# Seven block products in place of eight in the second feed-forward layer of a decoder block

## What is computed

```python
h2 = rms_norm(x, norm2_g[l])
x = x + jnp.square(jax.nn.relu(h2 @ w_ff1[l])) @ w_ff2[l]    # w_ff1 1024 x 4096, w_ff2 4096 x 1024
```

## Time and profile before

| | |
|---|---|
| median of 3 runs | 461.83 us (461.47 to 462.28) |
| the profiled execution itself | 461.82 us, span 459.7 us |
| PE busy | 452.8 us, 99% |
| DVE busy | 314.0 us, 68% |
| ACT busy | 239.2 us, 52% |
| POOL busy | 35.0 us, 8% |
| granted TensorE clock | 1.0 of full speed throughout |

### The profile page before, as it was taken

The page is one execution under the profiler, slowest core; times in us unless marked ns, Lnnn a source line. Parts: engine busy times, 40 slices in busy tenths (PEclk is TensorE's granted clock), DMA queues, the critical chain, the costliest instruction groups (busy, mean ns, idle before and its releaser), DMA issues.

```text
span 459.7 us, 8210 instructions
## 1 busy us (share of the span) xinstructions
PE 452.8 (99%) x3392; PEld 380.5 (83%) x3392; DVE 314.0 (68%) x438; ACT 239.2 (52%) x355; POOL 35.0 (8%) x44
## 2 busy tenths in 40 slices
PE   7999999999999999999999999999999999999997
PEld 4999988789977777878888888888888888888885
DVE  3868799675374867676688858766666666666662
ACT  5868584655565556666533547444444444444430
POOL 3003000023580001002000000000000000000000
PEclk9999999999999999999999999999999999999999
DMA  8973645433524434446656564656566555566402
GB/s 273 320 243 105 228 138 180 143 97 96 177 66 131 135 112 152 129 131 184 195 175 198 169 201 151 194 185 186 188 194 199 191 185 186 194 193 197 145 1 91
DMA packets 49076, 76.55 MB, mean 167 GB/s; under 512 B 3088, under 2 KB 29456, under 8 KB 49040
## 3 DMA queue, kind: packets, MB, share of 16 engines
q1 hardware_dynamic: 49040, 76.03, 53.1%
HBM read 74.97 MB, written 1.05 MB: 165 GB/s over the span
## 4 chain that ended last, share of the span: by engine, by line
PE 92%; DVE 4%; DMA 1%; ACT 1%; issue 1%; SPq 0%
PE bank L504 21%; PE bank L506 20%; PE bank L505 20%; PE bank L555 13%; PE bank L557 6%; DMA stage<-in_w_in 1%; PE bank L752 1%; PE bank L771 1%; PE bank L656 1%; DVE w_lo L1168 1%; DVE mat L1273 1%; DVE mat L1288 1%; DVE xs L1499 1%; PE bank L847 1%; PE bank L811 1%
## 5 line engine op out<-in xcount | busy, mean ns | idle before, releaser
L1168 DVE TENSOR_TENSOR w_lo<-stage,w_hi 128x1024 fp32r<-128x1024 f32 x138 | 167.6, 1223 | 82.7 <-ACT w_hi L918 82.5
L918 ACT CAST w_hi<-stage 128x1024 fp32r<-128x1024 f32 x138 | 144.1, 1052 | 126.3 <-PE bank L506 74.1
L555 PE MATMUL bank<-h_two,w_hi 128*128 128x512 f32 x256 | 91.2, 399 | 0.3 <-DVE h_two L1419 0.3
L557 PE MATMUL bank<-h_two,w_lo 128*128 128x256 f32 x256 | 71.8, 281 | 0.0
L504 PE MATMUL bank<-w_hi,h_two 128*128 128x512 f32 x144 | 59.8, 415 | 0.0
L555 PEld LDWEIGHTS bank<-h_two,w_hi 128*128 128x128 f32 x256 | 48.1, 188 | 12.3 <-issue 0.6
L504 PE MATMUL bank<-w_hi,r_hi 128*128 128x512 f32 x144 | 56.4, 392 | 0.0
L505 PE MATMUL bank<-w_lo,h_two 128*128 128x512 f32 x144 | 56.4, 391 | 0.0
L506 PE MATMUL bank<-w_hi,h_two 128*128 128x512 f32 x144 | 56.4, 391 | 0.0
L505 PE MATMUL bank<-w_lo,r_hi 128*128 128x512 f32 x144 | 56.2, 390 | 0.0
L506 PE MATMUL bank<-w_hi,r_lo 128*128 128x512 f32 x144 | 56.0, 389 | 0.0
(11 more groups left out here) (245 smaller groups left out, 630.5 us busy)
## 6 DMA issues: line engine op xcount, KB each, us to landing
stage<-in_w_ff SPq DMA_DIRECT2D x64, 512.0 KB, 3.7
stage<-in_w_in SPq DMA_DIRECT2D x54, 512.0 KB, 4.4
stage<-in_w_branch SPq DMA_DIRECT2D x12, 512.0 KB, 4.3
stage<-in_w_out SPq DMA_DIRECT2D x8, 512.0 KB, 4.4
xs<-in_x SPq DMA_DIRECT2D x2, 512.0 KB, 4.0
out<-xs SPq DMA_DIRECT2D x4, 256.0 KB, 2.1
cst<-in_consts SPq DMA_DIRECT2D x1, 608.0 KB, 6.0
lora<-in_g_up SPq DMA_DIRECT2D x1, 256.0 KB, 6.0
```

What stands on the lines that cost most here:

```text
L555: pe.matmul(o[:].rearrange("p (s t) -> p s t", s=2), wh[:, kk, cols], h_two[:, :, k], start=k == 0, stop=False)
L557: ins = pe.matmul(o[:, T:2 * T], wl[:, kk, cols], h_hi[:, k], start=False, stop=k == KD - 1)
L918: nc.scalar.copy(w_hi[:, v % RING], stage[:, v % STAGES]).then_inc(hi_done, 1)
L1168: dve.tensor_tensor(w_lo[:, v % RING], stage[:, v % STAGES], w_hi[:, v % RING].bitcast(F32), ALU.subtract)\
```

## The change

All 16 ff1 units now come first; their squared results all stay in SBUF (`fsq` has 16 buffers). Then come the 16 steps of the second layer. In seven of them (i = 0, 2, ... 12) the 2 x 2 by 2 x 2 block product is made by Winograd's form of Strassen's method, with seven block products and sums of blocks of both factors; such a step is two units, `("seven", i, 0)` and `("seven", i, 1)`, with four pieces. The first two are the loaded rows of `w_ff2` (of the first only half the columns is split), the other two (`SUMS`) are sums of weight blocks in the buffer `w_sum`, which isn't loaded but made by GpSimd. The other nine steps are as before. Products add up in eight PSUM banks, and DVE combines those after step 12.

The core of the diff:

```diff
-UNITS += [("ff1", 0)]
-for i in range(1, D_FF // 256):
-    UNITS += [("ff1", i), ("ff2", i - 1)]
-UNITS += [("ff2", D_FF // 256 - 1)]
+FF = D_FF // 256
+SEVEN = list(range(0, FF - 2, 2))
+UNITS += [("ff1", i) for i in range(FF)]
+for i in range(FF):
+    UNITS += [("seven", i, 0), ("seven", i, 1)] if i in SEVEN else [("ff2", i)]
...
+                if s >= STAGES:
+                    freed = LOADS[s - STAGES]
+                    sp.wait_ge(lo_done, freed + 1)
+                    if UNITS[freed // 2][0] == "seven":
+                        sp.wait_ge(wsum_ready, 4 * SEVEN.index(UNITS[freed // 2][1]) + 4)
...
+                elif u[0] == "seven":
+                    buf = 4 * (u[1] % 2)
+                    if u[2] == 0 and p == 0:
+                        pe.wait_ge(f_ready, SPLITS[u[1]])
+                    work = {(0, 1): ("M1", 0, 0, 0), (0, 2): ("M2", 1, 0, 0), (0, 3): ("M3", 3, 1, 1),
+                            (1, 0): ("M5", 2, 0, 0), (1, 1): ("M6", 2, 1, 1), (1, 2): ("M7", 3, 0, 0),
+                            (1, 3): ("M4", 1, 1, 1)}.get((u[2], p))
...
+            def gain(tt, c, ap):
+                xc = xs[:, tt, 512 * c:512 * c + 512]
+                return dve.scalar_tensor_tensor(out=xc, in0=ap, scalar=r2[:, tt:tt + 1], in1=xc, op0=ALU.mult, op1=ALU.add)\
+                          .then_inc(x_part, 1)
...
+                if (t, p) == (FF2_AT[SEVEN[-1] + 1], 2):
+                    dve.wait_ge(used, 2 * t)
+                    link(dve.tensor_copy(msum[0], ps(("mlp", "M1"))[:]))
+                    link(dve.tensor_tensor(msum[1], msum[0], ps(("mlp", "M6"))[:], ALU.add))
+                    link(dve.tensor_tensor(msum[2], msum[1], ps(("mlp", "M7"))[:], ALU.add))
+                    gain(0, 0, msum[0])
+                if (t, p) == (FF2_AT[SEVEN[-1] + 2], 2):
+                    dve.tensor_tensor(msum[3], msum[1], ps(("mlp", "M5"))[:], ALU.add).then_inc(tail_sum, 1)
+                    dve.tensor_tensor(msum[4], msum[2], ps(("mlp", "M5"))[:], ALU.add).then_inc(tail_sum, 1)
+                    gain(1, 0, msum[2])
+                    dve.wait_ge(tail_sum, 2)
+                    gain(0, 1, msum[3])
+                    gain(1, 1, msum[4])
...
+            for n, i in enumerate(SEVEN):
+                pool.wait_ge(sq_ready, i + 1)
+                if n >= 2:
+                    pool.wait_ge(f_ready, SPLITS[SEVEN[n - 2]])
+                a11, a21, a12, a22 = (fsq[i][:, P * b:P * b + P] for b in range(4))
+                s1, s2, s3, s4 = (a_sum[n % 2][:, P * b:P * b + P] for b in range(4))
+                pool.tensor_tensor(s1, a21, a22, ALU.add).then_inc(asum_ready, 1)
+                pool.tensor_tensor(s3, a11, a21, ALU.subtract).then_inc(asum_ready, 1)
+                pool.wait_ge(asum_ready, 4 * n + 2)
+                pool.tensor_tensor(s2, s1, a11, ALU.subtract).then_inc(asum_ready, 1)
+                pool.wait_ge(asum_ready, 4 * n + 3)
+                pool.tensor_tensor(s4, a12, s2, ALU.subtract).then_inc(asum_ready, 1)
+                v = 2 * FF2_AT[i]
+                if n >= 2:
+                    pool.wait_ge(lo_done, 2 * FF2_AT[SEVEN[n - 2]] + 4)
+                landed(pool, v)
+                landed(pool, v + 1)
+                b11, b12, b21, b22 = (source(v + r)[:, 512 * c:512 * c + 512] for r in range(2) for c in range(2))
+                t1, t2, t3, t4 = (w_sum[:, n % 2, r, 512 * c:512 * c + 512] for r in range(2) for c in range(2))
+                pool.tensor_tensor(t1, b12, b11, ALU.subtract).then_inc(wsum_ready, 1)
+                pool.wait_ge(wsum_ready, 4 * n + 1)
+                pool.tensor_tensor(t2, b22, t1, ALU.subtract).then_inc(wsum_ready, 1)
+                pool.tensor_tensor(t3, b22, b12, ALU.subtract).then_inc(wsum_ready, 1)
+                pool.wait_ge(wsum_ready, 4 * n + 2)
+                pool.tensor_tensor(t4, b21, t2, ALU.subtract).then_inc(wsum_ready, 1)
```

More of the change, by code:

```diff
@@ L65 @@
 UNITS += [("out", kh, ch) for kh in range(2) for ch in range(2)]
-UNITS += [("ff1", 0)]
-for i in range(1, D_FF // 256):
-    UNITS += [("ff1", i), ("ff2", i - 1)]
-UNITS += [("ff2", D_FF // 256 - 1)]
+FF = D_FF // 256
[3 more added lines that the diff above has]
+    UNITS += [("seven", i, 0), ("seven", i, 1)] if i in SEVEN else [("ff2", i)]
 SLOTS = len(UNITS)
 PIECES = 2 * SLOTS
+SUMS = [v for v in range(PIECES) if UNITS[v // 2][0] == "seven" and UNITS[v // 2][2] == 1]
+LOADS = [v for v in range(PIECES) if v not in SUMS]
+FF2_AT = [next(t for t, u in enumerate(UNITS) if u[0] in ("ff2", "seven") and u[1] == i) for i in range(FF)]
+FF2_END = FF2_AT[1:] + [SLOTS]
+SPLITS = [i + 1 + sum(n <= i for n in SEVEN) for i in range(FF)]
+SPLIT_AT = {FF2_AT[i - 1] if i else FF2_AT[0] - 1: i for i in range(FF)}
+M_BANK = {"M1": 0, "M2": 1, "M3": 2, "M5": 3, "M6": 6, "M7": 7, "M4": 4, "P22": 5}
+TAIL = [["M2", "M3"], ["M4", "P22"]]
 STAGES = 5
@@ L166, in plan_turns @@
                         use(("ff", u[1], j), 6 - 2 * (u[1] % 2) + j, dense=j == 1)
-                elif u == ("ff2", 0):
-                    for b in range(4):
-                        use(("mlp", b // 2, b % 2), b)
+                elif u == ("seven", 0, 0):
+                    for m, b in M_BANK.items():
+                        use(("mlp", m), b)
             for n in pe_uses(t, p):
@@ L343, in build_layer @@
         prob = [att[:, 384 * e:384 * e + 384] for e in range(2)]
[L344 removed]
+        ffs = [flat[:, 512 * i:512 * i + 512] for i in range(2)]
+        fsq = [big[:, i // 2, 512 * (i % 2):512 * (i % 2) + 512] if i < 12 else flat[:, 512 * (i - 10):512 * (i - 10) + 512]
+               for i in range(FF)]
+        msum = [flat[:, 3072 + 512 * i:3584 + 512 * i] for i in range(5)]
+        a_sum = [gg[:, 2 * i:2 * i + 2].rearrange("p k t -> p (k t)") for i in range(2)]
+        w_sum = ops[:].rearrange("p (i h n) -> p i h n", i=2, h=2)
         omu, oka, gq8 = small[:, 0:14], small[:, 14:18], small[:, 18:19]
@@ L434, in build_layer, with by_rows, piece_view, source @@
         sq_ready, f_hi, f_ready = sem("sq_ready"), sem("f_hi"), sem("f_ready")
+        asum_ready, wsum_ready, tail_sum, x_part = (sem(n) for n in ("asum_ready", "wsum_ready", "tail_sum", "x_part"))
         fin_ready, stored = sem("fin_ready"), sem("stored")
         block = ctx.enter_context(nc.Block())
-        def piece_view(buf, v, slots=RING):
+        def by_rows(row, v):
             kind = UNITS[v // 2][0]
-            k = {"feat": 4, "ff1": 4, "ff2": 1}.get(kind, 2)
-            return buf[:, v % slots].rearrange("p (k n) -> p k n", k=k)
+            k = {"feat": 4, "ff1": 4, "ff2": 1, "seven": 1}.get(kind, 2)
+            return row.rearrange("p (k n) -> p k n", k=k)
+        def piece_view(buf, v):
+            return by_rows(buf[:, v % RING], v)
+        def source(v):
+            if v in SUMS:
+                n = SUMS.index(v)
+                return w_sum[:, n // 2 % 2, n % 2]
+            return stage[:, LOADS.index(v) % STAGES]
+        def landed(eng, v):
+            if v in SUMS:
+                eng.wait_ge(wsum_ready, 2 * SUMS.index(v) + 2)
+            else:
+                s = LOADS.index(v)
+                eng.wait_ge(loaded[s % STAGES], 16 * (s // STAGES + 1))
+        def width(v):
+            u = UNITS[v // 2]
+            return slice(0, 512 if u[0] == "seven" and u[2] == 0 and v % 2 == 0 else 1024)
         def piece_dram(v):
```

74 lines of the change are left out of this document (46 added, 28 removed).

## The result

The changed kernel takes **475.56 us** (median of 4 runs, 474.94 to 476.11) where the kernel before took 461.74: a ratio of 1.0293 (1.0278 to 1.0309), **13.8 us more**. The forecast was 467.5, that is 5.7 us more than before; its range was 462 to 477. The profiled execution took 476.11 us.

What follows compares the result with a forecast made beforehand. PE bounds the kernel before; afterwards DVE, sharing turns with POOL, sets 12.5 us a pair. The second layer goes from 87.0 to 92.7 us, so 461.8 + 5.7 = 467.5 us, range 462 to 477.

Steps and rivals of the forecast that it cites:

- The bound and PE's saving: Whole kernel: PE sets the time before the change; seven steps of seven products save 21 matmuls, 4.76 us.
- Parting costs nothing: First layer run wholly ahead of the second: no matmul count changes, DVE's 4.3 us a unit hidden under PE's 5.66.
- DVE and POOL exclude each other and take turns: Second layer: DVE's splits and POOL's sums alternate, 12.5 us a pair against PE's 10.2; 464 to 471 us, chance 0.60.
- the hold of one sum: Time a POOL sum keeps DVE out: 0.87 us for 512 columns, 0.24 us for 128.
- Sums for the first two steps are made in the first layer, where DVE has room: Border between layers: these sums finish early, so PE ends the first pair at 10.2 us without a wait.
- From that split to the third pair: Second layer: from DVE's split for the second plain step at 11.2 us to PE's third pair at about 21.6.
- The end: From the seventh pair at 71.6 us, no sums remain; PE needs 21.1 us for it and the last two steps.
- Hidden: Rival: long sums shut DVE out hardly or not at all, PE stays the bound; 457.1 us, chance 0.12.
- DVE keeps its turn: Rival: POOL gets in only when DVE's queue is empty; 14.4 us a pair, 475 to 477 us, chance 0.09.
- Whole instructions exclude each other: Rival: each POOL sum holds DVE for its whole duration; 13.8 us a pair, 473 us, chance 0.12.
- Partly hidden: Rival: dead 0.07 us between splits and POOL's start-up overlap; pair near 11.5 us, 461 to 464 us, chance 0.07.
- What was to show it: Second layer about 92 us; 512-column sums mostly near 2 us, splits up to 2.1, PE waits some 2.3 in pairs 3 to 6.

Runs made afterwards that it cites:

- experiment 1: Against the changed kernel: layers parted only, all sixteen second-layer steps plain, no sums, no combination of banks; 461.43 us.
- experiment 2: Changed kernel with POOL's sums replaced by fills that write SBUF but read nothing, so the output is not the layer's; 455.63 us.
- experiment 3: Changed kernel with the four weight sums of each step of seven made by DVE, POOL keeping the four 128-column sums; 463.76 us.
- experiment 7: Changed kernel with one more 512-column sum by POOL in each step of seven, into a spare buffer; 482.91 us.
- experiment 4: Changed kernel with only four steps of seven products (0, 4, 8, 12), the other steps plain; 458.35 us.
- experiment 8: Changed kernel with POOL's four weight sums for the second step of seven replaced by fills, so the output is not the layer's; 471.57 us.

## Why the prediction was right in sign and short in size

- **The bound and PE's saving** were right. The 21 matmuls are 4.76 us, and with POOL's reads gone they show in full (82.4 against 87.2 us).
- **Parting costs nothing**: right (experiment 1), and PE is gapless through the first layer.
- **DVE and POOL exclude each other and take turns**: right for the bound, by the window, by experiment 2 (no reads, no cost), experiment 3 (weight sums moved to DVE, pairs of 11.6 in place of 13.5 us) and experiment 7 (one sum more, 1.10 us more). DVE's own 8.1 us a pair stood too.
- **The term that was mis-sized** is the hold of one sum. The forecast drew a line of 1.63 ns a column through sums of 16 and 256 columns and got 1.03 us for a 512-column sum, 0.87 of it against DVE. Measured are 1.29 (experiment 4) and 1.09. The sums of 16, 128 and 512 columns (0.22, 0.46 and 1.29 us) lie on one line of some 2.15 ns a column; the sum of 256 columns that was taken, `L1545` with 0.61 us, lies 0.13 under it. The trace of before held another sum of 256 columns, `L1554`, which took 0.74 us beside a DVE instruction with one input in PSUM (and 0.75 at 136.40):

```profile
118.42 0.74 POOL L1554 TENSOR_TENSOR ops<-ops 128x256 f32<-128x256 f32 x1
```

```profile
118.39 0.69 DVE L1295 TENSOR_TENSOR big<-bank,cst 128x512 f32<-128x512 f32 x1 [2.79 <-PE bank L752]
```

  A line through 0.22 and 0.74 us gives 1.29 us for 512 columns, as measured, and the hold by it 0.45 + 0.56 = 1.0 us, most of the way to 1.09. Why the two sums of 256 columns differ is open. The earlier trace rows was read too far for the same reason: its sum is an `L1554`, so the 0.59 us behind the split are not its whole duration. A pair takes 13.53 us and not 12.5, for three pairs **+3.1 us**. The bound of 1.22 us that the forecast gave for the duration was too low as well. (The Trainium skill, page "GPSIMD Engine Reference", section "Elementwise — side-by-side cycle accounting", gives 4497 ns for a sum of 2048 columns; by that an estimate is 2.2 ns a column, which agrees with the 2.15.)
- **The step of the walk that failed** is "Sums for the first two steps are made in the first layer, where DVE has room". The second of the two pieces that the sums read landed only at 366.25. POOL made the second step's sums from then to 374.1, across the border at 370.1, and held the last splits of the first pair's pieces with them:

```profile
366.25 2.25 POOL L1669 TENSOR_TENSOR ops<-stage 128x512 f32<-128x512 f32 x1 [1.72 <-DMA stage<-in_w_ff]
...
371.86 2.28 POOL L1674 TENSOR_TENSOR ops<-stage,ops 128x512 f32<-128x512 f32 x1
```

```profile
367.26 1.80 DVE L1242 TENSOR_TENSOR y_lo<-big,y_hi 128x512 fp32r<-128x512 f32 x1
368.98 1.77 DVE L1242 TENSOR_TENSOR y_lo<-gg,y_hi 128x512 fp32r<-128x512 f32 x1
370.67 2.32 DVE L1233 TENSOR_TENSOR w_lo<-ops,w_hi 128x1024 fp32r<-128x1024 f32 x1
372.91 1.27 DVE L1552 TENSOR_REDUCE mat<-bank 128x256 f32<-128x512 f32 x2
```

  The last reductions of the first layer, which the walk let begin at the border, began 2.8 us behind it, and the hidden split of the plain step with them. PE waited 0.75 and 1.64 us in the pair that was to be gapless, and everything behind it came later. DVE's first split for the second plain step began 14.3 us behind the border and not 11.2: **+3.1 us**, of which experiment 8 takes 2.4 away.
- **From that split to the third pair** 12.1 us passed in place of 10.4: **+1.7**. Three of the long sums and four short ones at the true price are 0.8 of it; the walk had also let the first sum run ahead of the split, while it held that split for 0.6. The third pair began 26.5 us behind the border, not 21.6.
- **The end** was as forecast: from the sixth to the seventh pair 12.46 us for 12.5, and 21.3 for 21.1 from there. The sum of the errors is 3.1 + 3.1 + 1.7 + 0.2 = 8.1 us, and 5.7 + 8.1 = 13.8.
- **Rivals.** "Hidden" fell with the 1.09 us. "DVE keeps its turn" came closest in total time (475 to 477 us), by luck: its pair is 14.4 us, and the 13.53 us of the changed kernel are DVE's own 8.1 and all eight holds, so POOL got in each time though DVE's queue was full. "Whole instructions exclude each other" came closest for the pair (13.8 us, 473 us in all), but by a wrong duration: a sum of 1.29 us holds DVE for 1.09, not for all of it, and whole instructions of 1.29 and 0.46 us would give a pair of 8.1 + 4 x 1.29 + 4 x 0.46 = 15.1 us. The rule of the Trainium skill's page "SBUF — State Buffer", that the first holds the other off for the whole instruction, is thus 0.2 us too long for each sum here. "Partly hidden" spoke of 0.07 us that are dead between splits; the earlier trace rows show none, splits of 1.22 us start 1.14 apart.
- **What was to show it** did: sums of 1.8 to 2.1 us on the mean for 1.29, splits up to 2.3 (forecast 2.1), waits of 1.5 to 2.8 us of PE (forecast 2.3). The means by line, POOL:

```profile
L1674 POOL TENSOR_TENSOR ops<-stage,ops 128x512 f32<-128x512 f32 x7 | 14.9, 2124 | 0.0
...
L1669 POOL TENSOR_TENSOR ops<-stage 128x512 f32<-128x512 f32 x7 | 12.5, 1789 | 72.4 <-DMA stage<-in_w_ff 72.4
```

## What to carry to other kernels

Work given to GpSimd isn't free for VectorE when both read SBUF and VectorE's instructions have two SBUF inputs: price it by what it takes from VectorE (here 1.09 us, against 0.63 on the mean if VectorE does the sum itself), and ask whether VectorE has that time in the stage at hand. A trade that relieves the bound engine pays only as often as the cover lasts: four steps of seven gave 3.4 us (2.7 of them by the second layer's length), seven cost 13.8. When a duration is extrapolated from smaller tiles, look at every undisturbed instruction of the kind that the trace has (here two of 256 columns, 0.61 and 0.74 us) and let the bounds take in what they disagree on. Ask in the walk when the inputs of the first rounds really land, and what stands ahead of the work that the bound engine waits for.

## What the runs showed of the hardware beyond this

**Turns are not certain.** In experiment 3 POOL's first short sum began 0.23 us into a split of DVE whose queue was full (DVE's next instructions are shown there), and came out only 5.99 us later:

```profile
403.02 5.99 POOL L1673 TENSOR_TENSOR gg<-big 128x128 f32<-128x128 f32 x1 [7.83 <-DVE y_lo L1259]
```

At DVE's handovers from 403.93 to 408.00 it did not get in. It did in the first gap, where DVE waited for its own result between 408.69 and 408.73. The same happened at 379.50, also for 5.99 us, while in the same run a like sum at 414.59 took 1.31 us. What decides it is open.

**The clock.** After the waits of 2.76 and 2.78 us PE ran for a while at half the granted clock (1.2 GHz of its two levels): the six matmuls behind 397.12 began 0.43 us apart in place of 0.23, and the window 390 to 400 shows a mean of 0.83. After waits of 1.47 and 1.48 us it stayed at full. The length of the wait alone doesn't decide it: in experiment 3 the clock was at 0.50 behind a wait of 1.93 us (window 381 to 384), in experiment 7 at 1.00 behind one of 2.67 (window 428.5 to 432).

```profile
397.54 0.63 PE L550 MATMUL bank<-w_hi,y_lo 128*128 128x512 f32 x1
397.97 0.63 PE L548 MATMUL bank<-w_hi,y_hi 128*128 128x512 f32 x1
```

It cost nothing in the changed kernel: the pairs with and without the slow stretch are 13.53 and 13.54 us long, since DVE sets them.

**Two lengths of the first layer.** Its 256 matmuls of 512 columns have a median of 391 to 395 ns in some profiled executions and of 398 in others, and the layer takes 89.9 or 91.5 us accordingly (experiment 2: from 277.0 to 366.9; experiment 4: from 277.2 to 368.7), with the same instructions. The ten runs of experiment 1 spread from 459.60 to 462.85 us, and their profiled execution, of 459.83, has the shorter length. A difference of medians under some 1.6 us can be this, and for that reason the second layer's length stands in the table. What sets the two lengths is open.
